# Moving a gate multiplication: expert activations weighed by GpSimd in the second expert loop instead of by GpSimd and VectorE in two loops

## The reference, cut to what matters

```python
def block(xb):
    ...                                     # top-16 of 128 x 128 product keys, 8 heads
    e = i1 * N_KEYS + i2                    # expert numbers, (tokens, 8, 16)
    gate = jax.nn.softmax(sc, axis=-1)
    h = jax.nn.gelu(jnp.einsum('bhkd,bd->bhk', peer_u[e], xb).astype(F32), approximate=False)
    return jnp.einsum('bhk,bhkd->bd', (gate * h).astype(xb.dtype), peer_v[e])
```

## Time and profile before

| | us |
|---|---|
| runs | 6142.63, 6141.86, 6152.51 |
| profiled execution, its own time | 6147.73 |
| its span | 6145.9 |
| PE busy | 5597.9 (91%) |
| DVE busy | 3725.9 (61%) |
| ACT busy | 2193.9 (36%) |
| POOL busy | 1346.6 (22%) |

### The profile page before, as it was taken

One profiled execution on the slowest core, in us unless ns is written; L12 is line 12 of the kernel. 1 busy time (PEld: TensorE's weight loads), 2 busy tenths in 40 slices (PEclk: granted clock), 3 DMA queues, 4 the chain that ended last, 5 costly groups with the idle time before them and its releaser, 6 DMA issues. The chain is left out here.

```text
span 6145.9 us, 109260 instructions
## 1 busy us (share of the span) xinstructions
PE 5597.9 (91%) x47164; PEld 5444.9 (89%) x47164; DVE 3725.9 (61%) x4902; ACT 2193.9 (36%) x2763; POOL 1346.6 (22%) x916
## 2 busy tenths in 40 slices
PE   8999999999999999899999991009999999999999
PEld 7888889999999999899999991009999999999998
DVE  5566543323277333568877770007777888988898
ACT  4333322222233322222343330003334555555555
POOL 0000000000022000006788888881110000000000
PEclk9999999999999999999999995559999999999999
DMA  3111122222267633214455551114445334344432
GB/s 98 48 38 55 43 89 90 105 89 104 78 217 244 204 105 136 90 62 105 103 134 121 122 124 2 0 0 148 151 150 184 112 129 156 125 146 168 140 139 88
DMA packets 289502, 682.61 MB, mean 111 GB/s; under 512 B 108705, under 2 KB 123937, under 8 KB 266145
## 3 DMA queue, kind: packets, MB, share of 16 engines
q1 hardware_dynamic: 187792, 618.99, 29.8%
q0 software_dynamic: 94208, 38.09, 5.3%
q10 hardware_dynamic: 7056, 19.00, 0.8%
HBM read 562.31 MB, written 113.67 MB: 110 GB/s over the span
## 5 line engine op out<-in xcount | busy, mean ns | idle before, releaser
L2331 POOL DMA_INDIRECT gate_rows<-ah_shares,ah_cells x640 | 1112.8, 1739 | 252.7 <-issue 198.3
L2724 PE MATMUL ps<-va_h_high,va_v_high 128*128 128x288 f32 x3584 | 1056.4, 295 | 11.4 <-DVE va_h_low L140 7.6
L2726 PE MATMUL ps<-va_h_high,va_v_low 128*128 128x288 f32 x3584 | 1057.8, 295 | 0.0
L2725 PE MATMUL ps<-va_h_low,va_v_high 128*128 128x288 f32 x3584 | 1056.5, 295 | 0.0
L2208 PE MATMUL ps<-ah_tsum,ah_uh 128*128 128x288 f32 x1248 | 369.9, 296 | 450.2 <-DVE ah_ul L140 450.2
L2724 PEld LDWEIGHTS ps<-va_h_high,va_v_high 128*128 128x128 f32 x3584 | 673.5, 188 | 12.2 <-DVE va_v_low L140 7.8
L2725 PEld LDWEIGHTS ps<-va_h_low,va_v_high 128*128 128x128 f32 x3584 | 673.5, 188 | 0.0
L2726 PEld LDWEIGHTS ps<-va_h_high,va_v_low 128*128 128x128 f32 x3584 | 673.4, 188 | 0.0
L2208 PEld LDWEIGHTS ps<-ah_tsum,ah_uh 128*128 128x128 f32 x1248 | 235.4, 189 | 450.5 <-DVE ah_ul L140 450.5
L140 DVE TENSOR_TENSOR ah_ul<-ah_u,ah_uh 128x1024 fp32r<-128x1024 f32 (+1 forms) x336 | 445.8, 1327 | 287.6 <-ACT ah_uh L2270 247.4
L2270 ACT CAST ah_uh<-ah_u 128x1024 fp32r<-128x1024 f32 x312 | 327.3, 1050 | 488.5 <-PE ps L2210 479.6
(11 more groups left out here) (491 smaller groups left out, 14125.0 us busy)
## 6 DMA issues: line engine op xcount, KB each, us to landing
ah_u<-peer_u SPq DMA_DIRECT2D x208, 512.0 KB, 5.7
va_v<-peer_v SPq DMA_DIRECT2D x96, 1024.0 KB, 5.4
ret_w<-w_ret SPq DMA_DIRECT2D x46, 1024.0 KB, 4.9
gate_rows<-mo_zeros POOLq DMA_DIRECT2D x128, 288.0 KB, 3.9
h_kept<-ah_h SPq DMA_DIRECT2D x128, 288.0 KB, 2.3
ah_hidden<-h_kept SPq DMA_DIRECT2D x60, 576.0 KB, 4.9
ah_v<-peer_v SPq DMA_DIRECT2D x30, 1024.0 KB, 5.0
rwkv_w<-w_rkv SPq DMA_DIRECT2D x24, 1024.0 KB, 4.8
```

Of the source, the lines that this page charges most:

```text
L2331: pool.indirect_dma_start(cell, bass.IndirectOffsetOnAxis(ap=cells[0:m, n, k:k + 1], axis=0), shares[0:m, n, k:k + 1], None, compute_op=AL ...
L2724: pe.matmul(z, ah[:, r, f], th[:, q, r, :], start=begin, stop=False, skip_group_check=True)
L2725: pe.matmul(z, ah[:, r, f], tl[:, q, r, :], start=False, stop=False, skip_group_check=True)
L2726: done = pe.matmul(z, al[:, r, f], th[:, q, r, :], start=False, stop=r == R - 1, skip_group_check=True)
```

## The change

- No row is weighed in the first loop as a pair is done. SP loads no gates there, and its wait for the 640 transfers is gone from pair 28. `keep` waits for gelu alone.
- The second loop takes the rows in order, from row 0. The first group (rows 0 to 7) is weighed at the end of the first stage by `weigh_first`: SP loads the hidden rows once product 2 of the last pair is done, then waits for product 3 and for all 640 transfers, and loads the gates. GpSimd multiplies the upper half of the rows (k = 0), VectorE the lower (k = 1), in two instructions of 128 x 1152 each.
- In the second loop READY is 1: groups 1 to 15 are weighed, all by GpSimd, eight instructions of 128 x 576 per group. VectorE and ScalarE wait on the counter `weighed`, where they worked themselves or waited for the load.
- Buffers are laid out anew: `hidden` moves in front of `v22`, the first of the four low parts of V (`al[0]`) gets a place of its own, and so does the fourth of the squares.

```diff
@@ gates_stage, SP
-            def gates(p, s):
-                if (p, s) == (UNWEIGHED, 1):
-                    for n in range(NTT):
-                        sp.wait_ge(scattered[n], 16 * SLOTS)
-                sp.dma_start(gate[s][:, :], K.gate_rows[PLAIN + 2 * p + s]).then_inc(gate_in[s], 16)
-
             def keep(p, s):
-                if p < UNWEIGHED:
-                    sp.wait_ge(gelu, PLAIN + 2 + 2 * p + 2 - s)
-                else:
-                    sp.wait_ge(weighed, 2 * (p - UNWEIGHED) + 2 - s)
+                sp.wait_ge(gelu, PLAIN + 2 + 2 * p + 2 - s)
...
-                for s in (1, 0):
-                    keep(p, s)
-                    if UNWEIGHED <= p + 1 < PAIRED:
-                        gates(p + 1, s)
+                if p < PAIRED - 1:
+                    for s in (1, 0):
+                        keep(p, s)
+            for x, to, source in ((2, K.hidden, K.h), (3, gate, K.gate_rows)):
+                sp.wait_ge(product, 7 * (PAIRED - 1) + x)
+                if x == 3:
+                    for n in range(NTT):
+                        sp.wait_ge(scattered[n], 16 * SLOTS)
+                for k in range(2):
+                    sp.dma_start(to[:, k, :, :], source[0:2 * R].rearrange("(r k) p t -> k p r t", k=2)[k])\
+                        .then_inc(hidden_and_gates_in[k], 16)
+            for s in (1, 0):
+                keep(PAIRED - 1, s)
@@ gates_stage, GpSimd and VectorE
-        def weigh(eng, p, s):
-            eng.wait_ge(gate_in[s], 16 * (p - UNWEIGHED) + 16)
-            eng.wait_ge(gelu, PLAIN + 2 + 2 * p + 2 - s)
-            eng.tensor_tensor(hs[:, s, :], hs[:, s, :], gate[s][:, :], ALU.mult).then_inc(weighed, 1)
+        def weigh_first(eng, k):
+            eng.wait_ge(hidden_and_gates_in[k], 32)
+            for h in range(2):
+                t = slice(HT * h, HT * h + HT)
+                eng.tensor_tensor(K.hidden[:, k, :, t], K.hidden[:, k, :, t], gate[:, k, :, t], ALU.mult)
+            eng.drain()
...
-            for p in range(UNWEIGHED, PAIRED - 1):
-                for s in (1, 0):
-                    weigh(pool, p, s)
+            weigh_first(pool, 0)
...
-            dve.wait_ge(weighed, 2 * (PAIRED - UNWEIGHED) - 2)
-            for s in (1, 0):
-                weigh(dve, PAIRED - 1, s)
+            weigh_first(dve, 1)
@@ finish_stage
-        READY = GROUPS - K.weighed_from // (2 * R)
+        READY = 1
 
         def row(g_):
-            return 2 * R * ((g_ + K.weighed_from // (2 * R)) % GROUPS)
+            return 2 * R * g_
...
+        @block.gpsimd
+        def _(pool):
+            for g_ in range(READY, GROUPS):
+                for k in range(2):
+                    pool.wait_ge(hg_in[k], landed(g_))
+                    for r in range(R):
+                        pool.tensor_tensor(b[:, k, r, :], b[:, k, r, :], g[:, r, :], ALU.mult).then_inc(weighed, 1)
...
                 if i == P1:
-                    if 0 < g_ < READY:
-                        dve.wait_ge(hg_in[1], landed(g_))
+                    if g_ >= READY:
+                        dve.wait_ge(weighed, weights_before(g_) + 2 * R)
                     turn(T3)
...
-                if i == P3 and READY <= g_ + 1 < GROUPS:
-                    dve.drain()
-                    for r in range(2, R):
-                        weigh(g_ + 1, r, 0)
                 if i == P4 and not last:
                     dve.drain()
-                    if nxt < READY:
-                        dve.wait_ge(hg_in[0], landed(nxt))
+                    dve.wait_ge(weighed, weights_before(nxt) + R)
                     turn(T1)
...
-                elif i == P6 and READY <= g_ + 1 < GROUPS:
-                    for r in range(2):
-                        weigh(g_ + 1, r, 0)
...
-                elif i == P4 and READY <= nxt < GROUPS:
-                    for r in range(R):
-                        weigh(nxt, r, 1)
-                    dve.drain()
```

More of the change, by code:

```diff
@@ L2572, in finish_stage @@
         values_at = at[0]
-        v12, v21, v22 = (room(n, [P, R, KD * P]) for n in ("v12", "v21", "v22"))
-        ah, al = (room(n, [P, R, KD * P], F32R) for n in ("v_high", "v_low"))
+        v12, v21 = (room(n, [P, R, KD * P]) for n in ("v12", "v21"))
+        al0 = room("v_low0", [P, KD * P], F32R)
         b = K.hidden
@@ L2577, in finish_stage @@
         at[0] += 8 * R * T
+        v22 = room("v22", [P, R, KD * P])
+        ah, al123 = room("v_high", [P, R, KD * P], F32R), room("v_low", [P, R - 1, KD * P], F32R)
+        al = [al0[:, :]] + [al123[:, r, :] for r in range(R - 1)]
         th, tl = (room(n, [P, 2, R, HT], F32R) for n in ("h_high", "h_low"))
@@ L2582, in finish_stage @@
         assert at[0] <= nc.sbuf_usable_end
-        squares = over("squares", [P, 4, KD, HT], values_at)
+        square_of = over("squares", [P, 3, KD, HT], values_at)
+        squares = [square_of[:, n] for n in range(3)] + [over("squares3", [P, KD, HT], b.manual_sbuf_range[0])[:, :, :]]
         rstd = over("rstd", [P, T], gates_at)
@@ L2662, in _ @@
             x1_quarter(2, acc[P4])
+            for v in range(2):
+                gates(READY, v, 0)
             def group(g_):
@@ L2680, in group @@
                     hidden(nxt, v, 1)
-                if nxt >= READY:
-                    sp.wait_ge(weighed, weights_before(nxt) + R)
-                    for v in range(2):
-                        gates(nxt, v, 1)
+                sp.wait_ge(weighed, weights_before(nxt) + R)
+                for v in range(2):
+                    gates(nxt, v, 1)
                 sp.wait_ge(v_low, n + 4 * P3 + 4)
@@ L2725, in product @@
                         pe.matmul(z, ah[:, r, f], tl[:, q, r, :], start=False, stop=False, skip_group_check=True)
[L2726 removed]
+                        done = pe.matmul(z, al[r][:, f], th[:, q, r, :], start=False, stop=r == R - 1,
                                          skip_group_check=True)
@@ L2742, in summed_squares @@
                         pe.wait_ge(squared, steps[c * len(steps) // KD])
-                    done = pe.matmul(SUM[:, quarter % 2, :], K.ones[:, :], squares[:, quarter, c, :],
+                    done = pe.matmul(SUM[:, quarter % 2, :], K.ones[:, :], squares[quarter][:, c, :],
                                      start=start and c == 0, stop=stop and c == KD - 1)
```

62 lines of the change are left out of this document (19 added, 43 removed).

## The result

| | before | after |
|---|---|---|
| runs beside each other, us | 6147.57 (6141.86 to 6158.61, 4 runs) | 5724.4 (5721.71 to 5729.48, 4 runs) |
| ratio after to before | | 0.9311, 95% interval 0.9294 to 0.9327 |
| profiled execution, its own time | 6147.73 | 5721.71 |
| its span | 6145.9 | 5719.9 |

The changed kernel is faster by 423 us. I had predicted 5756 with a range of 5736 to 5797, so the time lies 32 us under the forecast and 12 under the range. What I said would go went: the hole of 452.8 us. What I said the change would cost in return (50.6 at the seam, 14.3 behind it) was nearly twice what it did cost: 18.9 and 15.4. From here on I compare the profiled executions, as the prediction's sum did: 5760 there against 5721.71, 38 us.

A forecast was written before the change was run, and what follows sets the result against it. TensorE was taken as the bound outside one hole in the first loop. 6147.73 - 402 (shift) + 1.3 (clock) + 13 (GpSimd's weighings) = 5760 us for the profiled execution, 5756 for the median, range 5736 to 5797.

The forecast's parts named there:

- the hole of 452.8 us: First expert loop: TensorE's 450.2 us gap behind SP's wait for the gate transfers, plus 2.6 us at the lower clock, would go.
- the seam: Between the two expert loops: TensorE's idle time would grow from 7.6 to 58 us, leaving a shift of 402 us.
- the stages ahead of the change, to the first transfer: Everything before the first gate transfer: taken as before, 2825.2, with no room for it in the range.
- first transfer to the last, start to start: GpSimd's transfers into `gate_rows`: 2.22 us each beside the first loop, some 20 left when TensorE runs dry, the last beginning at 4257.
- last transfer to the issue of the gates' load: End of first loop: SP issues the gates' load 2.86 us after the last transfer's start, at 4260.
- landing of the gates, to the first weighing: End of first loop: two transfers of 1152 KB land at 4271, from a like pair's 10.9 us; bounds 4.9 and 15.
- weighing of the first group: End of first loop: GpSimd and VectorE take 8.1 us in turns, 5.4 side by side; 8 taken, to 4279.
- end of the block, and SP to TensorE: Between the loops: 0.4 us for the end of the block, then 2.9 us from SP to TensorE, which begins at 4282.4.
- second loop, with the clock's 1.3: Second loop: GpSimd's weighings delay VectorE, 0.9 us per group, 13 us over 15 groups; 1.3 us more for the lower clock.
- the walk through VectorE's rows: Second loop, products P6 and P4: adds 2.2 and 1.9 us late, 0.6 and 0.3 beyond what is free, 0.9 per group.
- The first rival: No loss in the second loop (13 us less) and up to 8 us off the seam: 5735 to 5745; chance 0.18.
- the second rival: Second loop: VectorE late in every group, adds blocked too or more lag; 3 us per group, 5788, or 5, 5818; chance 0.21.

## Why the prediction was wrong in its number

| step of the prediction | predicted | measured | share of the miss |
|---|---|---|---|
| the stages ahead of the change, to the first transfer | 2825.2, as before | 2817.9 | -7.3 |
| first transfer to the last, start to start | 1431.8 | 1404.0 | -27.8 |
| last transfer to the issue of the gates' load | 3 | 2.9 | -0.1 |
| landing of the gates, to the first weighing | 11 | 6.1 | -4.9 |
| weighing of the first group | 8 | 7.7 | -0.3 |
| end of the block, and SP to TensorE | 0.4 + 2.9 | 1.8 + 2.9 | +1.4 |
| second loop, with the clock's 1.3 | 1475.6 | 1476.7 | +1.1 |

The sum is -37.9 of the 38. The second row is the step that failed: the number of transfers left when TensorE runs dry, mis-sized by its rate.

**The step that failed** is this: "Beside a working VectorE there are 225 in 500 us, 2.22 us each", and with it "From 3705.3 to 4224.2 GpSimd does 519/2.22 = 233 of the 253. Some 20 are left when TensorE runs dry." The 225 were counted on transfers 128 to 384. Those belong to the second and third tile, 128 tokens each. The last 256 alternate between the fourth tile, 128 tokens, and the fifth, the 64 sample tokens. In the kernel before all but the first few of them fell into the hole, so no row showed them beside the loop. But the hole showed that there are two sizes (timeline of the kernel before):

```profile
3753.45 1.42 POOL L2331 DMA_INDIRECT gate_rows<-ah_shares,ah_cells  x1 [0.30 <-issue]
...
3755.18 1.56 POOL L2331 DMA_INDIRECT gate_rows<-ah_shares,ah_cells  x1 [0.30 <-issue]
```

One batch ends there and another begins. I read the 1.42 of the last one as the quiet duration of all, and took 2.22 for all beside the loop: one number from each side, neither for the mix that was left. At the measured 2.08 the last 256 take 533 us. Four transfers were left when TensorE stopped, and not 20. The code says which tile has 64 tokens, so part of the miss could have been foreseen.

The size alone is not all of it. Beside the loop a transfer costs its quiet duration, 0.30 us to the next one, and what it waits for a VectorE instruction in SBUF that it begins inside. Early in the loop that is 1.55 + 0.30 + 0.38 = 2.23 us. Among the last 256 it is 1.55 + 0.30 + 0.28 = 2.13 us for the batches of 128 tokens and 1.42 + 0.30 + 0.33 = 2.05 us for those of 64. So of the 0.14 us that the mix is quicker on average, about half is the smaller size of every second batch, and the other half is that its transfers wait less: of the batches of 128 tokens 45% begin inside such an instruction, where early in the loop it is 60%. The kernel with 64 tokens throughout waits 0.31 on average. I gave the count an uncertainty of -12 to +15 us, "if the count is off by ten, or the rate by 4%", when the rate was off by 6% over 256 transfers. That bound was no bound: it had no row of the other size in it.

**The landing** was mis-sized by 4.9 us. The nearest row was the hidden rows' own pair, 10.9 us. It had stood behind other loads; nothing was ahead of the first gates' load, and it landed in 6.0. The 14.8 of the kernel with 64 tokens shows the same load in company. The second, VectorE's, landed in 8.5, at 4233.75. My lower bound of 4.9, from the half size, held.

**The stages ahead** vary from run to run by more than this term: over these executions the first transfer begins between 2817.9 and 2830.1, a spread of 12 us. I gave it no room in the range. The medians show the same: 5724.4 and 5730.05 for one kernel.

**What was right.** The hole of 452.8 and its cause: putting back that wait alone restores 448.7. The second loop: 13 us predicted, 0.9 a group, and measured 1.0 a group and 15.4 in all with the clock's part (1.3 predicted for it). In P6 the walk through VectorE's rows gave an add 2.2 us late and 0.6 lost; measured are 2.3 and 0.66 (0.56 and the 0.10 behind it). P4 was to lose another 0.3 and lost nothing (its adds begin at 4790.73, 25.38 us behind P6's, while TensorE had been held up by 0.66 in between); instead 0.35 went to the low part of the third row in P6, which my walk had left out. So the total of a group, 0.9 predicted and 1.0 measured, is right in part by luck. The first rival's second half, no loss there, and the second rival, adds blocked as well, are both refuted, by the fifteen new pauses and by the 30 adds of 0.74 us inside weighings. Of the seam's other terms, the issue 2.9 us behind the last transfer and the start of TensorE behind SP (2.9, measured 2.86) held. The weighing in turns (8, measured 7.7) is right in part by luck: VectorE let GpSimd's first instruction go ahead because its own gates landed only at 4233.75, and only after that did the two engines meet, VectorE's first instruction taking 3.51 us instead of 1.35 beside GpSimd's second. The end of the block was 1.8 us and not 0.4, with GpSimd's drain.

The first rival named "up to 8 from the seam" and a time of 5735 to 5745. It was right in the sign of the seam's error, but the seam came out 32 us shorter than forecast, four times as much.

**What stays open.** What lengthens a transfer beside the loop is read from rows that have no exception; no run took VectorE's work away from a loop that went on. It is not settled why fewer of the mixed batches' transfers begin inside VectorE's instructions. A transfer's start depends on the one before, and both engines' patterns repeat, so a small change of size can shift which instructions are met; that is my reading. Nor was it tested what delays the last landing beside the hidden rows' loads.

## What to carry to other kernels

A rate taken from a stretch holds for the instructions of that stretch. Before it is carried over to what is left to do, look up what is left: its size, its number of tokens, what it alternates with, and what it waits for. And give a term that is a product of a rate and a large count a bound from the other size, not from a feeling.

A wait in an in-order queue costs what is queued behind it. Here 438 us hung on a wait that stood between loads of work that had nothing to do with it; at the end of the stage SP stands there for 20 us, and with batches that take turns for 9.

Giving work to an idle engine was no gain here, because the two engines take turns. GpSimd needs 2.4 us for what VectorE does in 0.75, and the low part that meets one weighing becomes 1.15 us longer. VectorE had room, so the work was free on it; on GpSimd it cost 15 us.

## What the runs showed of the hardware that I had not expected

- An indirect transfer's time on GpSimd depends on its number of tokens, but weakly: 1.42 us for 64 and 1.55 for 128 when quiet, one every 2.03 us and 2.23 us beside the first loop.
- An indirect transfer that begins while VectorE is inside an instruction with both operands in SBUF ends 1.42 us (128 tokens) or 1.29 us (64) after that instruction. One that begins ahead of such an instruction, or inside an add from PSUM, keeps its quiet duration (510 transfers of the kernel after and 502 of the one with 64 tokens, without exception).
- GpSimd's weighing is halved in width and takes 1.79 us instead of 2.42, its waits for its turn included; the new pauses of TensorE vanish with it.
- A load of 1152 KB landed in 6.0 us with none ahead of it and in 14.8 behind others, with the same instruction at the same place of the kernel.
- With 120 weighings of 0.75 us on GpSimd instead of on VectorE, VectorE's busy time was higher: 1096.0 of 1200 us, against 1079.8 with all of them on VectorE.
- A stage whose last work on GpSimd was a weighing ended 1.8 us behind VectorE's last instruction, and one without it 0.3 us behind.
